# Encoder trunk on one core: load order, a K-outer start of the input projection, adaLN moved between engines, index scores through PSUM

## The reference

```python
cond = jax.nn.silu(c)
mod = cond @ w_ada + b_ada                 # 1024 -> 6 x 1024
sh1, sc1, g1, sh2, sc2, g2 = split(mod, 6)
h = rms_norm(x, norm1_g) * (1.0 + sc1) + sh1
z = h @ w_in                               # 19 column tiles of 128
ya = gmlp(za); yb = dsa(zq, zk, zv, zqi, zki, zwi, rel_tab); yc = pool(zc); yd = swa(zdq, zdk, zdv, ...)
x = x + g1 * (concat(rms(ya), rms(yb), rms(yc), rms(yd)) * mix_out_g @ w_out)
h = rms_norm(x, norm2_g) * (1.0 + sc2) + sh2
x = x + g2 * conv_glu(h, w_up, conv_w, conv_b, w_down)
out = rms_norm(x, final_g)
```

```python
dots  = einsum('qhd,sd->qhs', qi, ki) * IDX_DIM ** -0.5           # 8 heads of 32
score = einsum('qh,qhs->qs', wi * IDX_HEADS ** -0.5, relu(dots))
idx   = top_k(score where admissible, 256)
```

## Time and profile before

| | us |
|---|---|
| median of 3 runs | 1412.76 |
| lowest and highest run | 1411.21, 1416.31 |
| span of the profiled execution | 1412.5 |
| TensorE busy | 1239.7 (88%) |
| VectorE busy | 904.3 (64%) |
| ScalarE busy | 556.9 (39%) |
| GpSimd busy | 595.9 (42%) |
| mean granted TensorE clock | 0.942 of 2.4 GHz |

### The profile page before, as it was taken

One profiled execution on the slowest core, in us unless ns is written; L12 is line 12 of the kernel. 1 busy time (PEld: TensorE's weight loads), 2 busy tenths in 40 slices (PEclk: granted clock), 3 DMA queues, 4 the chain that ended last, 5 costly groups with the idle time before them and its releaser, 6 DMA issues.

```text
span 1412.5 us, 17801 instructions
## 1 busy us (share of the span) xinstructions
PE 1239.7 (88%) x5618; PEld 1009.6 (71%) x5618; DVE 904.3 (64%) x1447; ACT 556.9 (39%) x953; POOL 595.9 (42%) x305
## 2 busy tenths in 40 slices
PE   2379888898878879999999998788889999999996
PEld 1267766677757758878878876587768888888874
DVE  3944999998763769979997996754542212221236
ACT  4233434423744245523431442463255423432442
POOL 1522222267320325545554555531435545554553
PEclk9689999999977989999999998899989999999997
DMA  8324455245013212222322323302213232323233
GB/s 303 134 93 160 165 180 153 92 142 189 17 31 134 74 55 94 96 97 90 104 89 90 103 89 120 119 16 78 101 45 104 90 104 90 104 89 99 95 104 119
DMA packets 56654, 150.10 MB, mean 106 GB/s; under 512 B 6137, under 2 KB 19833, under 8 KB 56609
## 3 DMA queue, kind: packets, MB, share of 16 engines
q1 hardware_dynamic: 37456, 123.02, 26.1%
q10 hardware_dynamic: 19152, 26.52, 5.8%
HBM read 138.99 MB, written 10.52 MB: 106 GB/s over the span
## 4 chain that ended last, share of the span: by engine, by line
issue 29%; DVE 27%; PE 27%; POOL 10%; ACT 4%; ACTq 1%; DVEq 1%; DMA 1%; POOLq 0%; SPq 0%
POOL w_lo L452 7%; PE ps L1325 7%; DVE score L1026 7%; PE ps L1326 7%; PE ps L1328 6%; DVE top L1020 5%; DVE score L1001 3%; POOL act_lo L581 2%; DVE conv_t L1250 2%; DVE w_ada L934 1%; PE ps L1508 1%; PE ps L1524 1%; PE ps L1484 1%; DVE h_lo L953 1%; PE ps L1535 1%
## 5 line engine op out<-in xcount | busy, mean ns | idle before, releaser
L452 POOL TENSOR_TENSOR w_lo<-w_raw,w_hi 128x1024 fp32r<-128x1024 f32 x173 | 419.7, 2426 | 617.1 <-ACT w_hi L598 617.0
L1325 PE MATMUL ps<-h_hi,w_hi 128*128 128x512 f32 x1008 | 402.5, 399 | 38.6 <-DVE h_lo L953 38.6
L1326 PE MATMUL ps<-h_lo,w_hi 128*128 128x512 f32 x1008 | 398.7, 396 | 0.0
L1328 PE MATMUL ps<-h_hi,w_lo 128*128 128x512 f32 x1008 | 372.8, 395 | 0.0
L598 ACT ACTIVATE w_hi<-w_raw 128x1024 fp32r<-128x1024 f32 x173 | 182.7, 1056 | 334.8 <-PE ps L1328 325.8
L1325 PEld LDWEIGHTS ps<-h_hi,w_hi 128*128 128x128 f32 x1008 | 192.9, 191 | 91.4 <-DVE h_lo L953 31.3
L1328 PEld LDWEIGHTS ps<-h_hi,w_lo 128*128 128x128 f32 x1008 | 192.7, 191 | 41.2
L1326 PEld LDWEIGHTS ps<-h_lo,w_hi 128*128 128x128 f32 x1008 | 193.4, 192 | 39.4
L1026 DVE MATCH_REPLACE8 score<-top,score 128x640 f32<-128x640 f32 (+1 forms) x192 | 166.2, 876 | 0.0
L1250 DVE SCALAR_TENSOR_TENSOR conv_t<-conv_in,conv_w,conv_t 128x512 f32<-128x512 f32 x44 | 62.6, 1422 | 159.3 <-ACT halo L891 159.3
L1020 DVE MAX8 top<-score 128x8 f32<-128x640 f32 (+1 forms) x192 | 158.4, 880 | 0.7
(11 more groups left out here) (169 smaller groups left out, 1476.4 us busy)
## 6 DMA issues: line engine op xcount, KB each, us to landing
w_raw<-in_w SPq DMA_DIRECT2D x173, 512.0 KB, 3.3
w_ada<-in_w_ada SPq DMA_DIRECT2D x32, 512.0 KB, 4.1
w_ada<-in_w_ada SPq DMA_DIRECT2D x8, 1024.0 KB, 7.4
x_sb<-in_x SPq DMA_DIRECT2D x4, 1024.0 KB, 10.2
bias<-f_dram ACTq DMA_DIRECT2D x2, 2048.0 KB, 9.9
x<-in_x ACTq DMA_DIRECT2D x2, 2048.0 KB, 7.7
out<-fin_o ACTq DMA_DIRECT2D x16, 256.0 KB, 2.2
q_st<-qk_dram ACTq DMA_DIRECT2D x24, 128.0 KB, 2.9
```

What stands on the lines that cost most here:

```text
L452: pool.tensor_tensor(r(w_lo[:, slot]), w_raw[:, slot], w_hi[:, slot], ALU.subtract).then_inc(w_lo_ready, 1)
L1325: pe.matmul(ps[:, bank], r(w_hi[:, slot, kk]), r(xh(kk)), start=first, stop=False)
L1326: pe.matmul(ps[:, bank], r(w_hi[:, slot, kk]), r(xl(kk)), start=False, stop=False)
L1328: mm = pe.matmul(ps[:, bank], r(w_lo[:, slot, kk]), r(xh(kk)), start=False, stop=last_k)
```

## The change

- SyncE issues x right behind c, then three parameter tensors, the adaLN weights in the order of use (shift and scale of one feature tile at a time, `w_ada0` with two slots), the first two units, and only then rel, onehot and the other parameters.
- The root is spread first, and ScalarE copies it to SBUF (rms_x). The row of relative biases is made behind it, and ScalarE no longer waits for its store before the squares.
- VectorE makes all first 16 adaLN tiles (`ada_tile(i, j)`), two per feature tile, between `scaled` (h_t, 1024 wide, from x and rms_x) and `rest` (h_lo, 1024 wide).
- Units 0 to 3 (N_FIRST) run K-outer: for each feature tile, TensorE runs the six matmuls of each of the four units, in all eight banks. Their split weights use three more places (w_first).
- The dots start two units later (DOT_UNIT = 5). Relu works in place in PSUM, relu_r is gone, and VectorE reads the scores from PSUM. Each dot waits until the score four places back is added.
- The later adaLN tiles leave VectorE: GpSimd multiplies them (`ada_products`, two per unit from unit 3 on), ScalarE sums them (`ada_sums(n-1)`, ahead of evac(n)). VectorE's top rounds are spread over 14 steps.
- Of the window sums, the scaling by 1/win moves from GpSimd to ScalarE (`pool_scale`), the second pair behind the fourth gMLP block, and the sums start at unit 14.
- The turns of the values use banks 4 to 7 by turns, after units 15 and 16.

The diff, cut (an added or removed empty line is left out):

```diff
--- before.py
+++ after.py
...
+        N_FIRST = 4
+        DOT_UNIT = 5
...
+        TOP_STEPS = N_IN - DOT_UNIT
+        early_steps = {step: 2 if step < DOT_STEPS else 4 if step < DOT_STEPS + 2 else 3
+                       for step in range(1, TOP_STEPS)}
         assert sum(early_steps.values()) == ROUNDS
...
+        def bank_of(n):
+            return 2 * (n if n < N_FIRST else n % 2)
...
-            sp.dma_start(rel[:], a["rel_bias"]).then_inc(rel_loaded, 16)
-            sp.dma_start(onehot[:], a["onehot"]).then_inc(rel_loaded, 16)
-            for name, dst in (("b_ada", b_ada), ("norm_g", norm_g), ("mix_g", mix_g), ("fin_g", fin_g),
-                              ("conv_w", conv_w), ("gm_b", gm_b), ("ident", ident), ("ws_t", ws_t),
-                              ("pool_c", pool_c)):
-                sp.dma_start(dst[:], a[name]).then_inc(params_loaded, 16)
-            sp.dma_start(sinks[:], a["sinks"].partition_broadcast(P)).then_inc(params_loaded, 16)
-            sp.dma_start(pool_s[:], a["pool_s"].partition_broadcast(P)).then_inc(params_loaded, 16)
             xs = a["x"].rearrange("(k p) s -> p k s", p=P)
             for i in range(4):
                 sp.dma_start(x_sb[:, 2 * i:2 * i + 2], xs[:, 2 * i:2 * i + 2]).then_inc(x_loaded[i], 16)
+            for name, dst in (("b_ada", b_ada), ("norm_g", norm_g), ("ident", ident)):
+                sp.dma_start(dst[:], a[name]).then_inc(first_params_loaded, 16)
...
+            def load_ada(i):
                 if i >= 2:
...
+                for j in range(2):
+                    sp.dma_start(w_ada0[:, i % 2, j], wa[:, KD * j + i]).then_inc(ada_w_first[i], 16)
+            load_ada(0)
+            load_ada(1)
+            load(0)
+            load(1)
...
+            load_ada(2)
+            load(2)
+            load_ada(3)
+            load(3)
+            for i in range(4, KD):
+                load_ada(i)
+            load(4)
+            load(5)
+            sp.wait_ge(unit_done, 2)
+            for n in range(ADA_UNIT, N_IN):
+                if n >= N_FIRST:
                     load(n + 2)
...
+                for c in (16 + 2 * (n - ADA_UNIT), 17 + 2 * (n - ADA_UNIT)):
+                    if c >= 18:
+                        sp.wait_ge(ada_rest_summed, c - 17)
+                    sp.dma_start(w_ada1[:, c % 2], wa[:, c]).then_inc(ada_w_rest[c % 2], 16)
...
+            for n in range(N_FIRST):
+                lo(n)
...
+            def ada_products(n):
+                for c in (16 + 2 * (n - ADA_UNIT), 17 + 2 * (n - ADA_UNIT)):
+                    pool.wait_ge(ada_w_rest[c % 2], 16 * (n - ADA_UNIT + 1))
+                    t = w_ada1[:, c % 2]
                     pool.tensor_tensor(t, t, cond[:], ALU.mult).then_inc(ada_weighted, 1)
...
                 lo(n + 1)
...
+                if n < U_V:
+                    query_key_lo(n)
+                ada_products(n)
...
+                    pool.wait_ge(pool_scaled, 2)
+                    pool_out(0, 0, win_a)
+                    pool_out(0, 64, win_b)
...
+            pool.wait_ge(pool_scaled, 4)
+            pool_out(1, 0, win_a)
+            pool_out(1, 64, win_b)
...
+            hi(0)
+            hi(1)
+            act.wait_ge(rms_spread, 1)
+            act.activation(rms_x[:], ps[:, 4:6].rearrange("p b c -> p (b c)"), ACT.Copy).then_inc(rms_kept, 1)
+            act.wait_ge(bias_row_made, 1)
+            act.activation(fbias[:].rearrange("p (a b) -> p a b", a=3), ps[0:8, 0:3, 0:384],
+                           ACT.Copy).then_inc(bias_row_out, 1)
+            act.wait_ge(bias_row_out, 1)
+            act.dma_start(f_dram.ap(), fbias[:]).then_inc(bias_row_stored, 16)
+            hi(2)
...
+            def h_tile(g):
+                act.wait_ge(norm_scaled, g + 1)
+                act.activation(r(h_hi[:, g]), h_t[:, g % 2], ACT.Identity, bias=mod[:, g:g + 1]).then_inc(norm_hi, 1)
+            h_tile(0)
+            hi(3)
+            for g in range(1, KD):
+                h_tile(g)
+            act.wait_ge(bias_row_stored, 16)
+            hi(N_FIRST)
...
-                    if i >= 4:
-                        act.wait_ge(scores_added, i - 3)
-                    act.activation(relu_r[:, i % 4, 0:n], ps[:, 4 + i % 4, 0:n], ACT.Relu,
+                    act.activation(ps[:, 4 + i % 4, 0:n], ps[:, 4 + i % 4, 0:n], ACT.Relu,
                                    scale=IDX_DIM ** -0.5).then_inc(relu_ready, 1)
...
+            def ada_sums(n):
+                for c in (16 + 2 * (n - ADA_UNIT), 17 + 2 * (n - ADA_UNIT)):
+                    act.wait_ge(ada_weighted, c - 15)
+                    t = w_ada1[:, c % 2]
+                    act.activation(t, t, ACT.Copy, accum_out=ada[:, c:c + 1]).then_inc(ada_rest_summed, 1)
...
+            evac(0)
+            evac(1)
+            store_index_queries(0)
+            evac(U_KIWI)
+            store_index_queries(1)
+            evac(U_Q)
+            hi(N_FIRST + 1)
+            act.wait_ge(qi_stored, 64)
+            for b in TOP_BLOCKS[:2]:
+                stack_queries(b)
...
+                ada_sums(n - 1)
+                if n == U_POOL + 2:
+                    act.wait_ge(pool_summed, 1)
+                    pool_scale(0, win_a, 2)
+                    pool_scale(64, win_b, 4)
                 evac(n)
...
+            ada_sums(N_IN - 1)
...
+                if b == 3:
+                    act.wait_ge(pool_summed, 2)
+                    pool_scale(0, win_a, 8)
+                    pool_scale(64, win_b, 16)
...
+            def ada_tile(i, j):
+                dve.wait_ge(ada_w_first[i], 32)
+                t, c = w_ada0[:, i % 2, j], KD * j + i
+                dve.scalar_tensor_tensor(out=t, in0=t, scalar=1.0, in1=cond[:], op0=ALU.mult, op1=ALU.mult,
                                          accum_out=ada[:, c:c + 1]).then_inc(ada_summed, 1)
+            def shift_scale(i):
+                dve.wait_ge(ada_summed, 2 * i + 2)
+                dve.tensor_tensor(mod[:, i:i + 1], ada[:, i:i + 1], b_ada[:, i:i + 1], ALU.add)
+                vlink(dve.scalar_tensor_tensor(out=scale_g[:, 0, i:i + 1], in0=ada[:, KD + i:KD + i + 1],
+                                               scalar=b_scale[:, i:i + 1], in1=norm_g[:, 0, i:i + 1],
+                                               op0=ALU.add, op1=ALU.mult))
+            def scaled(i):
+                if i >= 2:
+                    dve.wait_ge(norm_lo, i - 1)
+                    dve.wait_ge(norm_hi, i - 1)
+                dve.scalar_tensor_tensor(out=h_t[:, i % 2], in0=x_sb[:, i], scalar=scale_g[:, 0, i:i + 1], in1=rms_x[:],
+                                         op0=ALU.mult, op1=ALU.mult).then_inc(norm_scaled, 1)
+            def rest(i):
+                dve.wait_ge(norm_hi, i + 1)
+                dve.scalar_tensor_tensor(out=r(h_lo[:, i]), in0=h_t[:, i % 2], scalar=mod[:, i:i + 1], in1=h_hi[:, i],
+                                         op0=ALU.add, op1=ALU.subtract).then_inc(norm_lo, 1)
             vlink(dve.memset(sum_x[:], 0.0))
             add_squares(0, KD, sq_x, sum_x[:])
+            dve.wait_ge(first_params_loaded, 16 * 3)
+            vlink(dve.tensor_scalar(b_scale[:], b_ada[:, KD:2 * KD], 1.0, None, ALU.add))
+            dve.wait_ge(cond_ready, 1)
+            ada_tile(0, 0)
+            ada_tile(0, 1)
             root(0, diag_x[:], NBLK)
+            ada_tile(1, 0)
+            ada_tile(1, 1)
+            shift_scale(0)
+            dve.wait_ge(rms_kept, 1)
+            scaled(0)
+            for i in range(KD):
+                if i + 2 < KD:
+                    ada_tile(i + 2, 0)
+                rest(i)
+                if i + 2 < KD:
+                    ada_tile(i + 2, 1)
+                if i + 1 < KD:
+                    shift_scale(i + 1)
+                    scaled(i + 1)
+            dve.wait_ge(params_loaded, 16 * 8)
...
-                        dve.scalar_tensor_tensor(out=dst, in0=relu_r[:, i % 4, 0:n], scalar=wgt, in1=dst,
+                        dve.scalar_tensor_tensor(out=dst, in0=ps[:, 4 + i % 4, 0:n], scalar=wgt, in1=dst,
                                                  op0=ALU.mult, op1=ALU.add).then_inc(scores_added, 1)
...
             taken = 0
-            for step in range(ADA_STEPS):
+            for step in range(TOP_STEPS):
                 if step < DOT_STEPS:
                     accumulate(2 * step)
-                for c in (16 + 2 * step, 17 + 2 * step):
-                    ada_tile(c, w_ada1[:, c % 2], ada_w_rest[c % 2], 16 * (step + 1))
-                if step < DOT_STEPS:
                     accumulate(2 * step + 1)
...
+            over_features(0, KD, 4, sum_x, diag_x, NBLK)
+            pe.wait_ge(rel_loaded, 32)
+            for i in range(3):
+                last = pe.matmul(ps[0:8, i, 0:384], rel[:], onehot[:, 384 * i:384 * i + 384], start=True, stop=True)
+            last.then_inc(bias_row_made, 1)
             pe.wait_ge(bias_row_out, 1)
...
+            def first_units():
+                for kk in range(KD):
```

(20 more changed lines are left out.)

268 lines of the change are left out of this document (104 added, 164 removed).

## The result

The changed kernel takes 1370.75 us (median; 1367.66 to 1376.89) against 1412.62 of the kernel before in the same series: a ratio of 0.9715 (95% interval 0.9685 to 0.9745). The profiled execution has a span of 1369.0 us, 43.5 less than the 1412.5 of before.

The account below looks back on a forecast made before the run. VectorE was taken to bound the h stage and the dot units, then a loop of waits. Winning 45.5 us in the head and 4.3 in units 4 to 18, losing 7.1 in the seam, gave 42.7: 1370 us (1360 to 1382).

Parts of the forecast that it names:

- Head: From the start to the end of units 0 to 3: ends at 83.4 instead of 128.9, 45.5 us won.
- VectorE sets the pace: After the first h_lo, VectorE needs 5.35 us per K tile; TensorE needs 5.44 and stays dense.
- The rival of the low clock: TensorE stays at 1.2 GHz in the K-outer stage, eight bursts of 10.3 us: 1407 us; chance 0.07.
- Units 4 to 18: From the end of unit 3 to the end of unit 18: 4.3 us won, unit 18 ending at 288.5.
- the loop: Dot units 6 to 14: evacuation, relus, scores, top rounds, scores, last dot and matmuls wait in turn, up to 15.1 us.
- The products of unit 3, then qk_lo, then lo(5) end on GpSimd near 94.5, just in time: GpSimd's queue before unit 5: these three finish near 94.5 us, just in time.
- Seam: Behind unit 18: GpSimd's bunched work starts y<-ps,pool_s 20 us after unit 18 instead of 12.8, 7.1 us lost.
- The signs: Expected trace: bursts 5.4 us apart, PSUM scores 0.75, dots waiting for scores; wrong if dot units under 13 or over 17.
- The cover of w_lo: Per unit, GpSimd's 7 to 9.5 us stay hidden in some 14; otherwise w_lo is late and TensorE waits one for one.
- Relu in PSUM: In the dot units, ScalarE's relu of 512 elements within PSUM takes 0.6 us; if 1.2, a loop grows by 2.
- The rival that scores are not freed: Dot units: long scores do not come from GpSimd's SBUF traffic, 3.2 us more per unit, 1399 us; chance 0.06.
- An op with both inputs in SBUF queues with GpSimd; I add their times: VectorE beside GpSimd: such ops wait, so times add; one PSUM input frees them.

Follow-up runs that it names:

- run with the later wait: Changed kernel with ScalarE's wait for the stored index queries and the six loads behind it moved behind ada_sums(3), ahead of evac(4): 1365.17 us.
- run with earlier sums: Changed kernel with window sums and scalings after the first tile's sums one unit earlier, the last scalings ahead of evac(18): 1366.03 us.
- the base: The changed kernel itself, run again for comparison with the follow-up runs: 1371.56 us, ratio 0.9715 to the kernel before.

## Why the prediction was right

The predicted time (1370) is the measured one, and each of the three terms of its sum is within 2 us. That the total is so close is in part luck: the measured terms give 43.9 + 2.7 - 6.1 = 40.5 us where the prediction had 42.7, and the profiled span fell by 43.5. The missing 3 us lie behind the seam, in work that no edit touches.

- Head: predicted 45.5 won. Measured 128.9 - 85.05 = 43.9. The first h_lo starts at 36.5 and is ready at 38.9 (2.43 us long; 1.28 is the usual length), against 38.5 predicted. TensorE's first twelve matmuls, from 39.0 on, repeat every 0.43 us, the pitch of the 1.2 GHz level, though the profile gives a granted clock of 1.00 there; from 44.4 on it ran without a gap at 5.42 us per K tile. VectorE made a tile every 5.18 (h_t starts at 42.45, 47.62, 52.80 and so on), not 5.35. So the step "VectorE sets the pace" failed: TensorE did. The prediction's own prices say so: 5.44 a tile is more than 5.35, and seven bursts of 5.44 after the second tile at 47.0 end at 85.1, not 83.4. Both engines are so close that it cost 1.6 us. The load of x was summed too short as well: 4.7 MB at 423 GB/s and 3 us of latency, issued at 1.2, give 15.3 and not 14.5, and x landed at 15.6. The rival of the low clock came for half a burst only.
- Units 4 to 18: predicted 4.3 won, measured 209.4 - 206.7 = 2.7, but made of two errors that cancel in part. The dot units 7 to 14 took 115.5 us (129.98 to 245.50) where I had 118.5: the loop is 0.4 us a unit shorter than its summed links. Unit 6 ended at 130.0 instead of 123.2. Of these 6.8 us 2.4 stem from the later start of units 4 and 5. The other 4.4 are the step that I had called hidden: "The products of unit 3, then qk_lo, then lo(5) end on GpSimd near 94.5, just in time". That held for lo(5), and I did not carry the same queue one unit on. I had no price for 512 KB stores beside other traffic: qi_lo took 11.4 us where the index query stores took 2.6 to 4.7 before. Four of them and three loads, 3.5 MB, went at 285 GB/s between 84.0 and 96.6. The run with the later wait shows that ScalarE's stop for them caused TensorE's wait of 3.4 us: it fell to 0.3, though 1.6 us came back as a wait for the stacked queries.
- Seam: predicted 7.1 lost. Measured 18.9 - 12.8 = 6.1, with the window sums at 297.7 (297.3 predicted) and zc at 305.3 (304.5). Two errors cancel here too: products(18) ended at 293.2, not 291.5, and the two window sums behind them took 4.5 us, not 5.8. The run with earlier sums took back 3.2 us of this execution's 18.9, 4.4 of the base's 20.1, and 5.5 by the medians.
- The signs: bursts, scores, and the dots that wait for scores (7.5 us in 24 waits) are as forecast, and no dot unit took under 13 or over 17 us but unit 6 with its wait (18.1). One sign of being wrong came too. The prediction had said "Wrong if [...] w_lo appears among TensorE's waits", and w_lo appears once, with the 3.4 us before unit 6. The cover of w_lo failed in that one unit.
- Relu in PSUM: taken at 0.6, measured 585 ns (48 of them), against 599 to SBUF. Scores 0.75, measured 0.751. The rival that scores are not freed is refuted from both sides: in SBUF, beside the same work of GpSimd, they take 1827 ns.
- "An op with both inputs in SBUF queues with GpSimd; I add their times" was right in kind and too weak in size. In the experiment with relus in SBUF I priced a score at 1.15 by its mean of before, where GpSimd was busy 33.6 us in the dot units and not 74.1.
- From the start of y<-ps,pool_s to the end: 1058.4 us against 1061.3, 2.9 less. The change does not touch this work, and over the fourteen profiled executions of this study the same length runs from 1054.6 to 1061.4 us. So this is spread, and it is as large as some of the gains that are measured here.

"GPSIMD Engine Reference" in the Trainium skill (section 8) names the contention with VectorE instructions that have two SBUF inputs; the runs agree, 1827 and 1043 ns with GpSimd busy more and less, 751 with one input in PSUM. The dearer PSUM source of "VectorE: DVE Perf Modes" in the Trainium skill (section on the TRN2 errata), by an estimate from its table a fixed 65 ns, does not show. The scores with two tensor inputs have none of it: 751 ns against 752. In tensor_scalar PSUM is dearer, but by an amount that grows with the width: 479 against 344 ns for 256 elements, 608 against 408 for 384, 744 against 479 for 512. That is a lower rate and not a fixed extra, and the one tensor_scalar in eight scores makes it small here.

## What to carry over

When a profile shows the busiest engine at 92% and a change takes a third of its work away, sum the chain that goes round once per iteration before counting the gain: here the freed time was idle until one line on ScalarE (relus ahead of the evacuation) broke the loop, and that was worth as much as a third of the whole change. The sign of a part can hang on another part: adaLN on GpSimd costs 11 us with scores in SBUF, where its products slow the scores, and does not with scores in PSUM, where the kernel with it is 10 us faster. Read in the trace where such a gain lies before you name its cause: of these 10 us 5 are a late store, and none is in the dot units. A wait for a store in an engine's queue is priced by the traffic beside that store, and everything queued behind it, on every engine, comes with it.
